# Second stack's up slabs and the last head of the latent attention: twelve block slabs a layer instead of five, the convolution's taps on ScalarE, and four branch tiles moved

## The reference, cut to what matters

```python
def conv_ffn(xn, w_up, conv_w, conv_b, w_down):
    h = causal_depthwise_conv(xn @ w_up, conv_w) + conv_b    # 1024 -> 2 * 2816, three taps along the tokens
    g, u = jnp.split(h, 2, axis=-1)
    return (jax.nn.gelu(g) * u) @ w_down                      # 2816 -> 1024
```

## Time and profile before

| | |
|---|---|
| median of 3 runs | 2636.19 us (2635.64 to 2637.11) |
| the profiled execution | 2638.83 us, of which the span of the trace is 2637.0 us |
| TensorE busy | 2597.2 us, 98% |
| VectorE busy | 1736.7 us, 66% |
| ScalarE busy | 446.9 us, 17% |
| ups of the second stack | 149.4 us (layer 0, from 1938.6 us) and 149.2 us (layer 1, from 2407.5 us) |

### The profile page before, as it was taken

The page is one execution under the profiler, slowest core; times in us unless marked ns, Lnnn a source line. Parts: engine busy times, 40 slices in busy tenths (PEclk is TensorE's granted clock), DMA queues, the critical chain, the costliest instruction groups (busy, mean ns, idle before and its releaser), DMA issues.

```text
span 2637.0 us, 44746 instructions
## 1 busy us (share of the span) xinstructions
PE 2597.2 (98%) x18560; PEld 2366.9 (90%) x18560; DVE 1736.7 (66%) x3647; ACT 446.9 (17%) x857; POOL 160.4 (6%) x138
## 2 busy tenths in 40 slices
PE   9999999999999999999999999999999999999998
PEld 7889888778999999888878999987889999888998
DVE  4587675658677778675567666654577765366775
ACT  1011243221000100233331100013110011111000
POOL 0000000000430330000000231000000000000000
PEclk9999999999999999999999999999999999999999
DMA  9887432526446556532245444442334444343442
GB/s 381 308 333 269 160 113 81 187 109 239 168 169 234 197 217 226 214 144 81 106 175 191 167 163 175 158 171 103 128 144 156 157 166 171 127 144 124 156 154 95
DMA packets 74459, 459.00 MB, mean 174 GB/s; under 512 B 8308, under 2 KB 9216, under 8 KB 28176
## 3 DMA queue, kind: packets, MB, share of 16 engines
q1 hardware_dynamic: 73120, 449.28, 46.6%
q0 software_dynamic: 1136, 6.86, 0.7%
HBM read 455.01 MB, written 1.09 MB: 173 GB/s over the span
## 4 chain that ended last, share of the span: by engine, by line
PE 92%; DVE 4%; DMA 2%; DVEq 1%; issue 0%; ACT 0%; ACTq 0%
PE psum L592 15%; PE psum L834 15%; PE psum L768 14%; PE psum L675 9%; PE psum L651 8%; PE psum L1030 8%; PE psum L882 4%; PE psum L1086 3%; PE psum L1050 2%; PE psum L697 2%; DMA aring<-astream 2%; PE psum L978 1%; DVE aring L2031 1%; PE psum L789 1%; PE psum L710 1%; PE psum L1005 1%
## 5 line engine op out<-in xcount | busy, mean ns | idle before, releaser
L592 PE MATMUL psum<-h,ring 128*128 128x256 f32 x1184 | 259.7, 380 | 1.4 <-DVE arena L2005 0.8
L592 PEld LDWEIGHTS psum<-h,ring 128*128 128x128 f32 x1184 | 224.2, 190 | 33.4 <-ACT arena L1521 1.7
L834 PE MATMUL psum<-arena 128*128 128x128 f32 x2112 | 251.3, 277 | 2.2 <-DVE arena L1905 2.2
L834 PEld LDWEIGHTS psum<-arena 128*128 128x128 f32 x2112 | 244.2, 193 | 2.4 <-DVE arena L1905 2.4
L675 PE MATMUL psum<-aring,ring 128*128 128x256 f32 x1088 | 237.3, 380 | 1.7 <-issue 1.7
L1030 PE MATMUL psum<-h,ring 128*128 128x256 f32 x1024 | 235.4, 383 | 0.0
L675 PEld LDWEIGHTS psum<-aring,ring 128*128 128x128 f32 x1088 | 206.1, 190 | 29.5 <-issue 2.4
L1030 PEld LDWEIGHTS psum<-h,ring 128*128 128x128 f32 x1024 | 190.2, 190 | 30.0 <-issue 4.9
L834 PE MATMUL psum<-arena,ring 128*128 128x128 f32 x1584 | 191.6, 275 | 0.0
L834 PEld LDWEIGHTS psum<-arena,ring 128*128 128x128 f32 x1584 | 184.4, 192 | 0.2
L768 PE MATMUL psum<-arena 128*128 128x128 f32 x1440 | 170.6, 275 | 0.0
(11 more groups left out here) (489 smaller groups left out, 4089.8 us busy)
## 6 DMA issues: line engine op xcount, KB each, us to landing
ring<-wstream SPq DMA_DIRECT2D x349, 1024.0 KB, 4.8
aring<-astream SPq DMA_DIRECT2D x128, 512.0 KB, 4.9
arena<-astream SPq DMA_DIRECT2D x16, 512.0 KB, 18.2
arena<-wstream SPq DMA_DIRECT2D x3, 1024.0 KB, 20.5
arena<-decays POOLq DMA_DIRECT2D x2, 1024.0 KB, 5.7
sq<-decays POOLq DMA_DIRECT2D x2, 1024.0 KB, 4.8
kst<-const SPq DMA_DIRECT2D x1, 1216.5 KB, 8.6
x<-xT SPq DMA_DIRECT2D x1, 1024.0 KB, 4.8
```

The costliest lines, as they stand in the source:

```text
L592: mm = pe.matmul(out, lhsT=tile_at(at[0] % RING, t), rhs=rhs(k), start=k == 0, stop=k == kt - 1)
L834: mm = pe.matmul(out, lhsT=w, rhs=v, start=m == 0 and name in ("M1", "M5", "M3", "M4"), stop=m == NF // 2 - 1, skip_group_check=True)
```

## The change

Two independent edits.

**Ups of the second stack.** Block slabs are now 3, 4, 6, 7, 9, 10, 12, 13, 15, 16, 18 and 19: twelve a layer where there were five, so that from slab 3 on two block slabs and one plain one follow each other. From slab 3 on a slab's output lies in banks 2 * (s % 4) and the next one, where it may stay for three more slabs. Block slabs multiply `h`, which is `h2` already times the root (written by VectorE after slab 0, two instructions of 128x1024); their results need no factor any more and are put together straight into one of two buffers `convs`. Plain slabs go on with `h2` and `std`. The six tap multiplications go to ScalarE (one of the two biases with them), which writes three terms per slab; VectorE adds the three (two instructions of 128x512) one slab later, ScalarE then does the gelu, and VectorE multiplies the halves two slabs later (`gate`, without the bias). All buffers are doubled.

**Latent attention.** `FILL_BRANCH` takes one tile from each of steps 0 to 3 and puts these four into step 8. The 64 tiles are now full at 16, 32, 48 and 64 in steps 2, 4, 6 and 8, not in 1, 3, 5 and 7, so that the instruction that multiplies them into `gates` moves too.

```diff
-CONV_QUICK = (4, 7, 10, 13, 16)
+CONV_QUICK = (3, 4, 6, 7, 9, 10, 12, 13, 15, 16, 18, 19)
...
-FILL_BRANCH = (8,) * 8 + (0, 0)
+FILL_BRANCH = (7, 7, 7, 7, 8, 8, 8, 8, 4, 0)
...
-        cbuf = sb("cbuf", [P, 2, T + 3])
+        cvb = sb("cvb", [P, P + 2 * (T + 3)])
...
+        cbuf = cvb[:, P:].rearrange("p (a t) -> p a t", a=2)
+        convs = [cbuf, area(25680, 2, T + 3)]
+        u2_c11 = [cvb[:, 0:2 * (P + 3)].rearrange("p (a t) -> p a t", a=2)[:, :, 0:P],
+                  area(21000, 2, 2600)[:, :, 2083:2083 + P]]
...
+        conv_acc = [gate4[:, 2 * b:2 * b + 2] for b in range(2)]
+        taps_even = sq[:].rearrange("p (j a) t -> p j (a t)", a=2)
+        conv_terms = [[taps_even[:, j] for j in range(3)],
+                      [aring[:, 2, 0:2 * T], aring[:, 2, 2 * T:4 * T], condb[:, 0:2 * T]]]
...
-            def conv_pairs(layer, rhs, event, after):
+            def conv_pairs(layer, unscaled, scaled, event, after):
                 cnt.seen[event] += KD
                 for s in range(NF):
                     slot = at[0] % RING
                     slab_wait(at[0])
-                    if s >= 3:
-                        pe.wait_ge(bank_free, cnt.value("bank_free", s - 2))
-                    elif s == 0:
+                    if s == 0:
                         fresh()
+                    elif s >= 4:
+                        pe.wait_ge(bank_free, cnt.value("bank_free", {4: 2, 5: 3, 6: 3}.get(s, s - 3)))
                     if s in CONV_QUICK:
-                        if CONV_QUICK.index(s):
-                            pe.wait_ge(bank_free, cnt.value("bank_free", CONV_QUICK[CONV_QUICK.index(s) - 1] + 1))
+                        if s == CONV_QUICK[0]:
+                            pe.wait_ge(conv_tokens, layer + 1)
                         nth = len(CONV_QUICK) * layer + CONV_QUICK.index(s) + 1
-                        mm = block_products(slot, up_sums[:, nth % 2], 4, rhs, lambda: pe.wait_ge(conv_sums, nth))
+                        mm = block_products(slot, up_sums[:, nth % 2], 2 * (s % 4), scaled,
+                                            lambda: pe.wait_ge(conv_sums, nth))
                     else:
                         for n in range(2):
                             for k in range(KD):
                                 if s == 0 and n == 0:
                                     pe.wait_ge(sems[event], cnt.value(event, k + 1 - KD))
-                                mm = pe.matmul(psum[:, s % 4, n * T:(n + 1) * T],
-                                               lhsT=tile_at(slot, 8 * n + 4 * (k % 2) + k // 2), rhs=rhs(k),
+                                mm = pe.matmul(psum[:, s if s < 3 else 2 * (s % 4), n * T:(n + 1) * T],
+                                               lhsT=tile_at(slot, 8 * n + 4 * (k % 2) + k // 2), rhs=unscaled(k),
...
-            def gelu_gates(layer):
-                a = C2["cb"][0]
-                for s in range(NF):
-                    act.wait_ge(inputs_for_act, cnt.next("inputs_for_act"))
-                    E(gate4[:, 0], gate4[:, 0], ACT.Gelu_apprx_tanh, bias=p2[:, layer, a + s:a + s + 1]
-                      ).then_inc(functions_for_dve, 1)
+            def conv_gates(layer):
+                def par(name, off):
+                    a = C2[name][0] + off
+                    return p2[:, layer, a:a + 1]
+                for s in range(NF + 1):
+                    if s < NF:
+                        act.wait_ge(inputs_for_act, cnt.next("inputs_for_act"))
+                        for j in range(3):
+                            for a in range(2):
+                                bias = dict(bias=par("cb", 22 + s)) if j == 0 and a == 1 else {}
+                                last = E(conv_terms[s % 2][j][:, a * T:(a + 1) * T],
+                                         convs[s % 2][:, a, 1 + j:1 + j + T], ACT.Identity,
+                                         scale=par("cw", 44 * j + 22 * a + s), **bias)
+                        last.then_inc(functions_for_dve, 1)
+                    if s >= 1:
+                        act.wait_ge(inputs_for_act, cnt.next("inputs_for_act"))
+                        g = conv_acc[(s - 1) % 2][:, 0]
+                        E(g, g, ACT.Gelu_apprx_tanh, bias=par("cb", s - 1)).then_inc(functions_for_dve, 1)
             def cross(layer):
                 norm(KD, squared=True)
                 memory_attention()
                 norm(KD, squared=True)
-                gelu_gates(layer)
+                conv_gates(layer)
...
+                def terms_ready(s):
+                    dve.wait_ge(functions_for_dve, base + max(1, 2 * s))
+                def gate_ready(s):
+                    dve.wait_ge(functions_for_dve, base + min(2 * s + 3, 2 * NF))
+                def evacuate(s):
                     dve.wait_ge(slab_used, cnt.next("slab_used"))
+                    dst = convs[s % 2]
+                    at = s if s < 3 else 2 * (s % 4)
+                    if s not in CONV_QUICK:
+                        TT(dst[:, :, 3:], psum[:, at].rearrange("p (a t) -> p a t", a=2), both(std[:]), ALU.mult
+                           ).then_inc(bank_free, 1)
+                    else:
+                        low = psum[:, at]
+                        high = psum[:, at + 1].rearrange("p (a t) -> p a t", a=4)
+                        u2, u43, m1 = u2_c11[s % 2][:, 0:1], quads[:, 1:3], quads[:, 3:4]
+                        V.tensor_copy(quads[:, 3], low[:, 0:P])
                         D()
+                        TT(u2_c11[s % 2], m1.broadcast_to((P, 2, P)), low[:, P:3 * P].rearrange("p (a t) -> p a t", a=2),
+                           ALU.add)
+                        D()
+                        TT(u43, u2.broadcast_to((P, 2, P)), high[:, 1:3], ALU.add)
+                        D()
+                        TT(dst[:, :, 3 + P:], u43, high[:, 0:2], ALU.add)
+                        TT(dst[:, 1, 3:3 + P], quads[:, 2], low[:, 3 * P:], ALU.subtract).then_inc(bank_free, 1)
+                    D().then_inc(inputs_for_act, 1)
+                def gate(s):
+                    gate_ready(s)
+                    v = conv_acc[s % 2]
+                    TT(hidden[:, s], v[:, 1], v[:, 0], ALU.mult)
+                    if s % 4 == 3:
+                        D()
+                        token_sums(hidden, down_tokens, s // 2 - 1, 2)
+                    if s == NF - 1:
+                        D()
+                        token_sums(hidden, down_tokens, s // 2, 1).then_inc(weights_summed, 1)
+                def convolved(s):
+                    terms_ready(s)
+                    v, t = flat(conv_acc[s % 2]), conv_terms[s % 2]
+                    TT(v, t[0], t[1], ALU.add)
+                    D()
+                    TT(v, v, t[2], ALU.add).then_inc(inputs_for_act, 1)
+                V.memset(convs[1][:, :, 0:3], 0.0)
+                root_of_mean(KD * P)
+                base = cnt.value("functions_for_dve")
+                for s in range(NF + 2):
+                    if s < NF:
+                        evacuate(s)
+                    if s == 0:
+                        for a in range(0, KD, 4):
+                            TT(h[:, a:a + 4], h2[:, a:a + 4], both(std[:], 4), ALU.mult)
+                        D()
+                        token_sums(h, up_tokens, 0, 4).then_inc(conv_tokens, 1)
                     if s + 2 in CONV_QUICK:
                         sums_ahead(s + 2)
+                    if s >= 2:
+                        gate(s - 2)
+                    if 1 <= s <= NF:
+                        convolved(s - 1)
+                    if s in (18, 20):
+                        D()
+                        weight_sums(first + NF, s // 2 - 9)
+                cnt.seen["functions_for_dve"] += 2 * NF
```

30 lines of the change are left out of this document (4 added, 26 removed).

## The result

The changed kernel takes 2623.46 us (median of 6 runs, 2622.38 to 2626.48); the kernel before took 2636.89 us beside it (6 runs, 2635.64 to 2639.51). The ratio is 0.9949, 95% interval 0.9937 to 0.9961: faster by 13.4 us. The prediction was 2623.6.

The account below looks back on a forecast made before the run. TensorE's work was taken to bound the kernel, except for its wait on VectorE at the last head. 9.24 us from the ups plus 3.4 from the last head, 12.6 us, brought the 2636.19 us median to 2623.6; range 2621.5 to 2629.

Parts of the forecast that it names:

- Ups, TensorE: Second stack's ups: seven more block slabs in each of two layers, 0.66 us shorter each, 9.24 us less.
- Dear short products: Rival, ups: 128-token products cost more, 10.0 us a block slab, kernel at 2676 us; chance 0.01.
- Ups, VectorE: Ups: VectorE needs 17.7 us per three slabs against TensorE's 19.41 and keeps up, 1.7 us to spare.
- VectorE busy for about nine tenths: Sign of being right, ups: VectorE's expected busy share, after a computed occupation of 91%.
- Start and end: Ups: slab 3's sums ready at 1955.9, needed at 1960.0; at the end, sums fit the down projection by 2 us.
- ScalarE: Ups: scalings and gelu take 3.0 us, perhaps 3.6 with handings over, of 6.47 us a slab; it keeps up.
- The open question of the table: Ups, ScalarE: whether scalings between gelus load a table; one 1.28 us load a layer taken, two a slab the upper bound.
- Last head: End of latent attention: four moved tiles fill TensorE's 1.81 us wait a layer; gain 3.4 us.
- the 0.1 us for the moved instruction and the shortened steps: Latent attention: loss a layer from the later product into `gates` and seven-tile steps, booked within 0 to 0.3 us.
- Small waits: Rival, ups: a few block slabs wait for weight sums, one us at five places, 2629 us; chance 0.08.
- a last head without gain: Rival, latent attention: seven-tile steps wait for VectorE as long as step 8 did, 2627 us; chance 0.07.
- VectorE as pacemaker: Rival, slabs 3 to 21: longer VectorE instructions set the pace, 38 us more, 2662 us; chance 0.05.

Follow-up runs that it names:

- the extra instruction: The changed kernel with one more VectorE instruction of 128x512 a slab in the ups, its result read by nobody; 2628.1 us (1 run).
- the kernel with eight tiles: The changed kernel with FILL_BRANCH (6, 6, 6, 6, 8, 8, 8, 8, 8, 0), eight tiles in step 8 instead of four; 2626.3 us (one run).

## Why the prediction was right

The mechanism was right in both parts. That the number came within 0.2 us is in part luck: the parts add up to 13.1 us and not 12.6, and the kernel before, which was 2636.19 us in the prediction, was 2636.89 beside the changed one.

**Ups, TensorE.** 9.24 us booked, 9.1 found. The 0.66 us a slab is rounded; 4.57 / 7 is 0.653. Dear short products had no part in it: 6.25 us a block slab holds in pairs, in fives and in twenties.

**Ups, VectorE.** The step was right, its terms a little high. Start to start the trace of after has 2.12 us for putting a block slab together (2.07 booked), 0.83 for a plain one (0.79), 2.75 for weight sums (2.91), 1.37 for two additions of the terms (1.46), 0.34 for the halves (0.42) and 1.8 for token sums: 2 x 2.12 + 0.83 + 2 x 2.75 + 3 x 1.37 + 3 x 0.34 + 0.75 x 1.8 = 17.05 us of 19.41, against 17.7. That the rest is 2.4 and not 1.7 us agrees with the extra instruction, which fitted with room left. One sign that I announced was wrong: "VectorE busy for about nine tenths". It is busy for 111.85 of 144.80 us, 77%, and for 16.20 of 19.40 in the middle, 84%. Occupation from start to start counts the gaps between dependent instructions (when a block slab is put together, an instruction that needs the one before starts 0.07 us after its end), the busy time doesn't, and the first three slabs have less to do.

**Start and end.** Slab 3 was to have its token sums at 1955.9 before a start at 1960.0, 4.1 us in hand; it had 5.3, because two scalings of 128x1024 took 2.36 us and not 3.4. At the end nothing waited in `down`, and the kernel with the taps on VectorE shows that this is where a debt would have been paid.

**ScalarE.** Six scalings take 2.60 us and the gelu 0.51, 3.1 us a slab (3.0 to 3.6 booked). The open question of the table has its answer in one load a layer: the scalings did not bring one.

**Last head.** Right in its mechanism and undersized: 3.4 us booked (within bounds of 2.8 to 3.6), 4.0 found. Two things were mis-sized. The profile's idle time of 1.81 us leaves out what instructions overlap: before the wait, TensorE's last L1008 pair starts 0.22 us before it could have gone on (585.41 + 0.22 = 585.63), and it went on at 587.61, so the wait cost 1.98 us from start to start, and some 0.06 us behind it, as after each wait in the kernel with eight tiles. And the 0.1 us for the moved instruction and the shortened steps wasn't there: before the projection TensorE waits 0.54 us where it waited 0.52, and in step 3 the weights were ready at 557.16 and fetched at 557.34, 0.18 us in hand, where I had 0.09. The kernel with eight tiles shows how near it is: with six tiles the early steps wait.

**The rivals.** Small waits, a last head without gain and VectorE as pacemaker did not come. The last needs more work on VectorE than this change gives it: the taps in place of the additions (2.44 for 1.37 us a slab) or weight sums for every slab bring it about, 0.6 us more a slab don't. ScalarE beside it did not stretch VectorE's instructions: 128x512 stayed at 0.68 to 0.69 us. No rival and no term named the clock: a long wait can cost more than its length, by products at the lower level behind it. It did not touch the stages that the prediction was about, because they had no such wait left.

## What to carry to other kernels

When one engine sets the pace and another has slack, cost the second in distances from start to start, step by step, including where its debt would fall due; busy shares understate how full it is and the averages hide the due date. Moving work to an idle engine is worth nothing in itself, only as the room that it makes for shorter work on the engine that sets the pace. Before work goes to GpSimd, look at whether VectorE's instructions beside it take two operands from SBUF. A wait is worth the distance by which the next start moves, which can be a tenth more than the idle time shown; and look at the granted clock behind it.
